# One more mixed pair in the turn of the FFN loop, and low parts made two chunks at a time

## What is computed

```
h = rmsnorm(x, norm_ffn_g[l])
x = x + (jax.nn.silu(h @ w_gate[l]) * (h @ w_up[l])) @ w_down[l]
return rmsnorm(x, norm_final_g)
```

## Time and profile before

| | |
|---|---|
| median of three runs | 1094.39 us |
| the profiled execution's own time | 1094.19 us |
| its span, first to last instruction | 1092.1 us |
| TensorE (PE) busy | 1080.7 us, 99% of the span |
| VectorE (DVE) busy | 936.1 us, 86% |
| ScalarE (ACT) busy | 601.1 us, 55% |
| mean granted clock of TensorE | 0.998 |
| chain that ended last | PE 80%, DVE 13%, DMA 3% |

### The profile page before, as it was taken

The page is one execution under the profiler, slowest core; times in us unless marked ns, Lnnn a source line. Parts: engine busy times, 40 slices in busy tenths (PEclk is TensorE's granted clock), DMA queues, the critical chain, the costliest instruction groups (busy, mean ns, idle before and its releaser), DMA issues.

```text
span 1092.1 us, 15574 instructions
## 1 busy us (share of the span) xinstructions
PE 1080.7 (99%) x5386; PEld 892.1 (82%) x5386; DVE 936.1 (86%) x1043; ACT 601.1 (55%) x738; POOL 189.9 (17%) x322
## 2 busy tenths in 40 slices
PE   9999999999999999999999999999999999999997
PEld 7878778888988888888888888888888888888886
DVE  7999998754875788989898998989899898989987
ACT  7569544445753565545555464655546465555544
POOL 7130143320100320311030302003030300303011
PEclk9999999999999999999999999999999999999999
DMA  9884588864665677666576666658566665757662
GB/s 360 286 232 147 179 235 242 268 191 150 212 218 187 205 221 229 214 206 212 197 230 220 185 228 204 201 191 241 200 210 214 207 206 182 229 192 231 214 213 113
DMA packets 123802, 232.18 MB, mean 213 GB/s; under 512 B 12016, under 2 KB 19568, under 8 KB 123120
## 3 DMA queue, kind: packets, MB, share of 16 engines
q1 hardware_dynamic: 113392, 215.10, 61.1%
q0 software_dynamic: 9952, 15.62, 5.4%
q10 hardware_dynamic: 416, 0.92, 0.2%
HBM read 218.09 MB, written 5.11 MB: 204 GB/s over the span
## 4 chain that ended last, share of the span: by engine, by line
PE 80%; DVE 13%; DMA 3%; issue 2%; ACT 1%; DVEq 0%; POOL 0%; SPq 0%; POOLq 0%; ACTq 0%
PE ps L1787 36%; PE ps L1751 31%; DVE w_lo L941 4%; PE ps L1778 3%; PE ps L1771 3%; PE ps L1775 3%; DMA raw<-in_w_in 2%; DVE w_lo L947 1%; DVE wb L1074 1%; DVE wb L1072 1%; ACT w_hi L544 1%; DVE wb_t L1073 1%; PE ps L2095 1%; PE ps L2096 1%; PE ps L2097 1%
## 5 line engine op out<-in xcount | busy, mean ns | idle before, releaser
L550 ACT ACTIVATE w_hi<-raw 128x1024 fp32r<-128x1024 f32 (+1 forms) x166 | 156.7, 955 | 191.2 <-PE ps L1787 117.7
L544 ACT ACTIVATE w_hi<-raw 128x1024 fp32r<-128x1024 f32 x135 | 142.7, 1060 | 154.0 <-DMA raw<-in_w_in 53.2
L941 DVE TENSOR_TENSOR w_lo<-raw,w_hi 128x1024 fp32r<-128x1024 f32 x136 | 163.8, 1220 | 63.7 <-ACT w_hi L544 63.1
L424 POOL DMA_DIRECT2D ff_moved<-ff_turned x184 | 97.0, 536 | 601.7 <-DVE ff_turned L1365 543.3
L947 DVE TENSOR_TENSOR w_lo<-raw,w_hi 128x1024 fp32r<-128x1024 f32 (+1 forms) x166 | 176.3, 1088 | 23.7 <-ACT w_hi L550 22.9
L550 ACT ACTIVATE w_hi<-raw_more 128x1024 fp32r<-128x1024 f32 x82 | 84.5, 1054 | 54.9 <-PE ps L1751 36.5
L947 DVE TENSOR_TENSOR w_lo<-raw_more,w_hi 128x1024 fp32r<-128x1024 f32 x82 | 97.4, 1218 | 8.4 <-ACT w_hi L550 8.4
L559 ACT ACTIVATE mix_hi<-mix 128x1024 fp32r<-128x1024 f32 x80 | 83.5, 1056 | 21.9 <-DVE mix L1312 15.2
L1323 DVE TENSOR_TENSOR mix_lo<-mix,mix_hi 128x2048 fp32r<-128x2048 f32 x40 | 91.4, 2285 | 0.0
L1751 PE MATMUL ps<-w_hi,ffT_hi 128*128 128x512 f32 x320 | 85.6, 389 | 0.0
L1751 PE MATMUL ps<-w_lo,ffT_hi 128*128 128x512 f32 x320 | 85.6, 389 | 0.0
(11 more groups left out here) (362 smaller groups left out, 2238.4 us busy)
## 6 DMA issues: line engine op xcount, KB each, us to landing
raw<-in_w_in SPq DMA_DIRECT2D x79, 512.0 KB, 5.4
raw<-in_w_gate SPq DMA_DIRECT2D x68, 512.0 KB, 3.9
raw<-in_w_up SPq DMA_DIRECT2D x68, 512.0 KB, 4.6
raw<-in_w_down SPq DMA_DIRECT2D x46, 512.0 KB, 4.1
raw_more<-in_w_down SPq DMA_DIRECT2D x42, 512.0 KB, 4.5
raw<-in_w_out SPq DMA_DIRECT2D x32, 512.0 KB, 4.1
raw_more<-in_w_gate SPq DMA_DIRECT2D x20, 512.0 KB, 4.5
raw_more<-in_w_up SPq DMA_DIRECT2D x20, 512.0 KB, 5.5
```

The lines of the kernel that those rows point to most:

```text
L424: eng.dma_start(moved[32 * b:32 * b + 32, :, a].rearrange("p t k j -> p t (k j)"), turned[32 * a:32 * a + 32, b].rearrange("p t k j -> p t ...
L544: nc.scalar.activation(w_hi[:, n % SPL], raw[:, n % RAW], ACT.Copy).then_inc(S["high_done"], 1)
L550: nc.scalar.activation(w_hi[:, c % SPL, at], raw_of(c)[:, at], ACT.Copy).then_inc(S["high_done"], 1)
L941: tt(w_lo[:, n % SPL], raw[:, n % RAW], w_hi[:, n % SPL].bitcast(F32), ALU.subtract).then_inc(S["low_done"], 1)
```

## The change

- `UNITS` becomes "CSCSSCSS": pair 7 is mixed too, so there are five mixed pairs and three plain ones, and a mixed pair is the last of the turn. The two slots of `mix_hi` and `mix_lo` go by `q % NM % 2`, so the first mixed pair of a turn takes the same slot as the last one of the turn before, and waits until that is free.
- The sums of h for pair 7 get a place of their own (`sD_hi`, `sD_lo`), `s_sum` gets two more blocks, and `combos` makes them for any mix of two pairs: for the last column two mixed pairs.
- The banks are numbered anew. Down columns 0 and 2 use P1's bank and bank 7, columns 1 and 3 those of P6 and P7 (`COL_BANKS`). Chunk 16 waits for ScalarE's copy of P1 (`p1_ready`), chunk 18 for the sums of P6 and P7 (`sum_step`). Pair 1 waits for the third add to `x2`, and only its second half for the fourth.
- `first_product` waits for the first half of the last mixed pair, pair 7, and `first_sums` waits for `mix_free` of that pair, which is given by its last matmul.
- `loop_low_two` makes the low parts of two chunks in one instruction of 128 x 2048 and then adds two to `low_done`. It is used for the plain pairs and for chunks 18 and 19, and 22 and 23.

```diff
-UNITS = "CSCSSCSC"
+UNITS = "CSCSSCSS"
...
-B_P2, B_P3, B_P4, B_P5, B_P1, B_P6, B_P7 = range(7)
+B_P2, B_P3, B_P4, B_P5, B_P6, B_P7, B_P1 = range(7)
+COL_BANKS = ((B_P1, 7), (B_P6, B_P7))
...
-             ("sC_hi", [P, 4, 2, P], F32R), ("sC_lo", [P, 4, 2, P], F32R)],
+             ("sC_hi", [P, 3, 2, P], F32R), ("sC_lo", [P, 3, 2, P], F32R), ("sD_hi", [P, 4, P], F32R), ("sD_lo", [P, 4, P], F32R)],
...
+        def combo_parts(c):
+
+            first, parts = 0, []
+            for u in (2 * c, 2 * c + 1):
+                width = 4 if u in MIXED else 2
+                to = [s_mixed[part][MIXED.index(u)] if u in MIXED else s_plain[part][PLAIN.index(u)] for part in range(2)]
+                parts.append((s_sum[:, first:first + width], to))
+                first += width
+            return parts
...
+        def column_psum(col):
+            a, b = COL_BANKS[col % 2]
+            return ps[:, a:b + 1]
...
                     if turn is not None and step == 1:
-                        act.wait_ge(S["mix_free"], count(turn, NM, q))
-                    nc.scalar.activation(mix_hi[:, q % 2, half_], mix[:, half_], ACT.Copy).then_inc(S["mix_high"], 1)
+                        act.wait_ge(S["mix_free"], count(turn, NM, q + (NM % 2 and q == NM)))
+                    nc.scalar.activation(mix_hi[:, q % NM % 2, half_], mix[:, half_], ACT.Copy).then_inc(S["mix_high"], 1)
...
             def first_product(j):
 
-                act.wait_ge(S["mix_free"], j * NM + (NM + 1))
+                act.wait_ge(S["pe_done"], j * TURN + (LOOP0 + 2 * MIXED[-1] + 1))
                 act.wait_ge(S["mix_low"], j * NM + NM)
...
             def first_sums(j):
 
                 dve.wait_ge(S["p1_ready"], j + 1)
+                dve.wait_ge(S["mix_free"], j * NM + (NM + 1))
                 tt(mix[:, 1], ps[:, B_P6], mix[:, 0], ALU.add).then_inc(S["sum_step"], 1)
...
+            def loop_low_two(c, turn=None):
+
+                dve.wait_ge(S["high_done"], count(turn, TURN, LOOP0 + c + 2))
+                s = c % SPL
+                tt(w_lo[:, s:s + 2], raw_pairs[c // 2 % (RING // 2)], w_hi[:, s:s + 2].bitcast(F32), ALU.subtract
+                   ).then_inc(S["low_done"], 2)
+
             def pair_low(c, turn=None):
 
-                loop_low(c, turn)
                 if mixed_pair(c):
+                    loop_low(c, turn)
                     loop_low(c + 1, turn, slice(NCOL, CK))
                     mix_low(c, turn)
                 else:
-                    loop_low(c + 1, turn)
+                    loop_low_two(c, turn)
...
                 first_sums(j)
                 last_sums(j)
-                loop_low(d + 2, j)
-                loop_low(d + 3, j)
+                loop_low_two(d + 2, j)
                 ff(j + 2)
...
                 loop_low(d + 5, j)
-                loop_low(d + 6, j)
-                loop_low(d + 7, j)
+                loop_low_two(d + 6, j)
                 down_add(j, 1)
...
+                if u == MIXED[0]:
+                    pe.wait_ge(S["cols_added"], turn * 4 + 8)
                 pe.wait_ge(S["mix_low"], count(turn, NM, q + 1))
...
                     if u == MIXED[0]:
                         pe.wait_ge(S["ff_ready"], j + 1)
-                        pe.wait_ge(S["cols_added"], j * 4 + 8)
+                        pe.wait_ge(S["cols_added"], j * 4 + 7)
...
                     if c == 2 * GRP:
                         pe.wait_ge(S["ffT_lo_ready"], j + 1)
+                        pe.wait_ge(S["p1_ready"], j + 1)
+                    if c == 2 * GRP + 2:
                         pe.wait_ge(S["sum_step"], j * 4 + 2)
```

More of the change, by code:

```diff
@@ L239, in build @@
             [("zT", [P, 8, SEQ], F32), ("sqT", [P, 8, SEQ], F32), ("y1T", [P, 8, SEQ], F32)],
-            [("mix_hi", [P, 2, 4, NCOL], F32R), ("mix", [P, 4, NCOL], F32), ("s_sum", [P, 6, P], F32)],
+            [("mix_hi", [P, 2, 4, NCOL], F32R), ("mix", [P, 4, NCOL], F32), ("s_sum", [P, 8, P], F32)],
             [("x_gain", [P, TOK, D_MODEL], F32)],
@@ L254, in build @@
             s_mixed[part] += [x[:, i] for i in range(2)]
+        for part in range(2):
+            s_mixed[part].append(s_last[part][:])
         wbT, dec, sT = (m[k] for k in ("wbT", "dec", "sT"))
@@ L572, in combo_high @@
                 act.wait_ge(S["s_summed"], c + 1)
-                i, k, _ = column_combos(c)
-                nc.scalar.activation(s_mixed[0][i], s_sum[:, 0:4], ACT.Copy).then_inc(S["s_hi"], 1)
-                nc.scalar.activation(s_plain[0][k], s_sum[:, 4:6], ACT.Copy).then_inc(S["s_hi"], 1)
+                for sums, (hi, _) in combo_parts(c):
+                    nc.scalar.activation(hi, sums, ACT.Copy).then_inc(S["s_hi"], 1)
             def xh(r):
@@ L1277, in combos @@
             def combos(c):
-                _, _, one = column_combos(c)
                 pair = h_sum[:].rearrange("p (u k) (t s) -> p u k t s", u=2, t=TOK)
-                (a11, a21), (a12, a22) = ([pair[:, one, k, t] for t in range(TOK)] for k in range(2))
-                plain = pair[:, 1 - one]
-                dve.wait_ge(S["h_summed"], 3 * c + 1)
+                done = sum(1 + 2 * (u in MIXED) for u in range(2 * c)) - c
+                dve.wait_ge(S["h_summed"], done + 1)
                 if c:
@@ L1285, in combos @@
                     dve.wait_ge(S["s_lo"], 2 * c)
[L1286 to L1292, removed]
+                mixed = []
@@ new lines, in combos @@
+                for i, (sums, _) in enumerate(combo_parts(c)):
+                    if 2 * c + i in MIXED:
+                        a11, a21, a12, a22 = (pair[:, i, k, t] for k in range(2) for t in range(TOK))
+                        tt(sums[:, 0], a21, a22, ALU.add).then_inc(S["h_summed"], 1)
+                        tt(sums[:, 2], a21, a11, ALU.subtract)
+                        mixed.append((sums, a11, a12))
+                    else:
+                        last = tt(sums, pair[:, i, :, 0], pair[:, i, :, 1], ALU.subtract)
@@ L1294, in combo_low @@
+                for i, (sums, a11, _) in enumerate(mixed):
+                    dve.wait_ge(S["h_summed"], done + 2 + i)
+                    tt(sums[:, 1], sums[:, 0], a11, ALU.subtract).then_inc(S["h_summed"], 1)
+                for i, (sums, _, a12) in enumerate(mixed):
+                    dve.wait_ge(S["h_summed"], done + 2 + len(mixed) + i)
+                    last = tt(sums[:, 3], a12, sums[:, 1], ALU.subtract)
+                last.then_inc(S["s_summed"], 1)
             def combo_low(c):
-                i, k, _ = column_combos(c)
@@ L1297, in combo_low @@
                 dve.wait_ge(S["s_hi"], 2 * c + 2)
-                tt(s_mixed[1][i], s_sum[:, 0:4], s_mixed[0][i].bitcast(F32), ALU.subtract).then_inc(S["s_lo"], 1)
-                tt(s_plain[1][k], s_sum[:, 4:6], s_plain[0][k].bitcast(F32), ALU.subtract).then_inc(S["s_lo"], 1)
+                for sums, (hi, lo) in combo_parts(c):
+                    tt(lo, sums, hi.bitcast(F32), ALU.subtract).then_inc(S["s_lo"], 1)
             def mix_sums(c, turn=None):
@@ L1322, in mix_low @@
                 dve.wait_ge(S["mix_high"], count(turn, 2 * NM, 2 * q + 2))
-                tt(mix_lo[:, q % 2], mix[:], mix_hi[:, q % 2].bitcast(F32), ALU.subtract).then_inc(S["mix_low"], 1)
+                tt(mix_lo[:, q % NM % 2], mix[:], mix_hi[:, q % NM % 2].bitcast(F32), ALU.subtract).then_inc(S["mix_low"], 1)
             def first_sums(j):
                 dve.wait_ge(S["p1_ready"], j + 1)
+                dve.wait_ge(S["mix_free"], j * NM + (NM + 1))
                 tt(mix[:, 1], ps[:, B_P6], mix[:, 0], ALU.add).then_inc(S["sum_step"], 1)
@@ L1378, in down_col @@
                 dve.wait_ge(S["cols_added"], before)
-                b0 = 6 - 2 * (c % 2)
                 cols = x2[:, :, NCOL * c:NCOL * (c + 1)]
-                tt(cols, ps[:, b0:b0 + 2], cols, ALU.add).then_inc(S["cols_added"], 1)
+                tt(cols, column_psum(c), cols, ALU.add).then_inc(S["cols_added"], 1)
             def side(n):
@@ L2112, in _ @@
                 ready(n)
-                column_chunk(n, n % SPL, act_pair(8 * part + 2 * i), 2 * (c % 2), i == 0, i == 3)
+                column_chunk(n, n % SPL, act_pair(8 * part + 2 * i), (2 * (c % 2), 2 * (c % 2) + 1), i == 0, i == 3)
                 side(n)
```

16 lines of the change are left out of this document (7 added, 9 removed).

## The result

The changed kernel takes **1110.51 us** (median of four, 1109.50 to 1111.75) beside 1094.10 for the kernel before: a ratio on record of 1.0143, interval 1.0131 to 1.0156 (the two medians alone give 1.0150). It is slower by 16.4 us; forecast were 1106 and a range of 1099 to 1111. The profiled execution took 1111.34 with a span of 1109.2, 17.1 over the span before.

What follows compares the result with a forecast made beforehand. TensorE bounded the kernel before; a VectorE loop was to pace the changed one: 6.71 + 10.88 + 1.29 + 45.14 = 64.02 us a turn against 62.84. Turn 0's +1.1 and nine turns' +10.6 gave +11.7, about 1106 us, range 1099 to 1111.

Steps and rivals of the forecast that it cites:

- the chain: From line 1328 (now 1348) to chunk 18's start: four sums 4.37, merged low part 2.29, hand-over 0.05, together 6.71 us.
- The stall at chunk 18: TensorE waits 1.47 us each turn for chunk 18's low part, ready at T + 6.86, wanted at T + 5.44.
- T: Start of TensorE's down stage (chunks 16 to 23); VectorE was forecast to reach line 1328 (now 1348) some 0.5 us later.
- The merged low part: Low parts of two chunks in one VectorE instruction: taken as 2.29 us alone, 2.20 to the next start, from mix_lo.
- VectorE's stretch: From the merged low part of chunks 24 and 25 to line 1328 (now 1348), VectorE without pause: 45.14 us.
- The rule against mergers: Broken-up instructions finish work sooner: separate lows would start chunk 18 some 1.07 us earlier; the opposite rule saves 0.07 each.
- The loop: Chunk 18 through chunk 21's end, VectorE's low part and back to line 1328: 64.02 us a turn, setting the pace.
- Rival 4: VectorE later still: deadlines of pairs 4 and 7 missed, gaps between instructions, 0.5 us a turn more, 1111 us; chance 0.12.
- covered by idle time like that before 419.10: Ahead of the loop: the extra column sums, some 0.3 us of VectorE, were to fall into idle time.
- Rival 5: The clock falls for the stalls: one chunk a turn at 1.2 GHz, 2.72 us more each, 1133 us; chance 0.03.
- The likeliest case: The forecast itself: a turn of 64.02 us set by the loop through VectorE, about 1106 us; chance 0.61.
- Rival 1: VectorE stays ahead and only TensorE's 0.68 us a turn shows: 1087.6 us, faster; chance 0.06.

Runs made afterwards that it cites:

- e8: Changed kernel with the low parts of pairs 0 and 2 in two instructions each again, chunks 18 and 19 still merged: 1104.83 us.
- e1: Changed kernel with the low parts of chunks 18 and 19 in two instructions again, nothing else: 1099.21 us.
- e3: Changed kernel with the low parts of the next turn's pair 0 (chunks 24 and 25) in two instructions again: 1108.39 us.
- e2: Changed kernel with all five merged low parts in two instructions each again, leaving the fifth mixed pair alone: 1095.19 us.
- e4: Kernel before, pair 7 still plain, with merged low parts for its four plain pairs, chunks 18, 19 and 22, 23: 1096.22 us.
- e9: Kernel before with merged low parts for its plain pairs and chunks 22, 23, but chunks 18 and 19 separate: 1095.12 us.
- e6: Changed kernel reordered: merged low 18, 19 before the sums, chunk 20's high part before SiLU, pairs 0 and 2 separate: 1087.97 us.
- e5: Changed kernel with the merged low part of chunks 18 and 19 made ahead of the four sums, nothing else: 1109.70 us.

## Why the prediction was right, and where it was short

**What bounds, and the chain.** The stall at chunk 18 behind sums and merged low part was forecast at 1.47 with TensorE leading and is 1.48 there (e8); in the changed kernel line 1348 starts 0.39 after T, not 0.5. The chain itself was summed to 6.71 and is 6.72 (604.60 to 611.32). The merged low part, priced from mix_lo, takes 2.28 (608.98 to 611.26). VectorE's stretch from the low part of chunk 24 to line 1348, forecast 45.14, is 668.88 - 623.71 = 45.17.

**The rule against mergers.** The Trainium skill (Perfetto Trace Analysis, Optimizing Scalar/DVE Operations) gave two opposite rules. The one on broken-up instructions is what the runs follow (e1: 11.3 us back). The saving by the other, forecast 0.07 an instruction, shows in the start-to-start times (2.20 for 634.71 to 636.91, 2.27 before), and bought nothing. The Trainium skill (VectorE: DVE Perf Modes, The TRN2 errata) has a formula for a float32 addition of two tensors that gives 2.29 us for 2048 elements, an estimate, and the trace agrees for this subtraction: 2.28 to 2.29.

**The loop, step mis-sized.** Forecast 64.02 a turn, measured 64.33 (64.28 in the turn shown). The term that was short is the one from chunk 18's start to VectorE's low part of chunk 24: 10.88 + 1.29 = 12.17 was taken from a TensorE that doesn't start behind a wait; it is 12.39 (611.32 to 623.71), of which 0.15 is in the matmuls. The other 0.07 lies between the start of chunk 22 and VectorE's low part (622.35 to 623.71, 1.36 where 1.29 was taken). Over nine turns this (2.0), 0.03 a turn in VectorE's stretch (0.3) and 0.47 us that line 1356 idled once in the last turn make 2.8 us. That a second loop of the same length (pair 2, e3) lay under the first was not seen; it doesn't alter the time, but made an experiment fail.

**Rival 4** (VectorE later still, 1111) came nearer to the time than the forecast did, but not by its cause. Its missed deadlines of pairs 4 and 7 are there, and cost the weight loads up to 0.3 us each; yet VectorE's own stretch is 45.17 of 45.14, so they don't lengthen the loop. What did is the term above.

**The turn ahead.** The passes begin at 478.8, 0.8 later than the forecast gives (476.9 + 1.1 = 478.0). The step that failed is "covered by idle time like that before 419.10": the sums for pair 7 belong to the last column, behind that idle time.

```profile
428.27 0.69 DVE L1318 TENSOR_TENSOR sB_lo<-s_sum,sB_hi 128x512 fp32r<-128x512 f32 x1
428.87 0.69 DVE L1318 TENSOR_TENSOR sD_lo<-s_sum,sD_hi 128x512 fp32r<-128x512 f32 x1
429.67 2.29 DVE L1490 TENSOR_TENSOR w_lo<-raw,w_hi 128x2048 fp32r<-128x2048 f32 x1
432.84 1.23 DVE L1331 TENSOR_TENSOR mix<-raw 128x1024 f32<-128x1024 f32 x1 [0.87 <-DMA raw<-in_w_up]
```

Pair 0's low part starts at 429.67; it was 428.83 in the kernel before. Of the 0.84, 0.37 is there already when the last low part ahead of these starts (427.12, 426.75 before; it waits for ScalarE's high part, which stands behind the sums and their high part, 0.61 where it was 0.40), and 0.47 comes behind it, 0.27 of that by the longer low part of the sums (0.69, where it was 0.42). The mergers aren't the cause: in e2, which has none, pair 0's low part starts at 429.69. And e4 and e9, which have the mergers without the fifth mixed pair, begin at 476.6 and 477.4.

**The clock.** Rival 5 had the right mechanism and the wrong place: the clock stayed at 2.4 GHz through nine stalls of 1.5 us and fell once, behind the last turn's stall. That stall was the longest, 2.03 us, since line 1356 came 0.47 late. Of the 1.8 us that the end behind the last pass of line 1359 is longer (51.4 against 49.6), the clock is 1.55, the slow start 0.15 and 0.1 is the start of chunk 18 behind that pass. In e3, with 1.69 of idle at the same place and no half clock, the time behind the last pass is 49.8. Only one of the four executions of the changed kernel left a trace. Their mean granted clocks, 0.997, 0.999, 0.999 and 0.998 for 1111.34, 1109.69, 1109.50 and 1111.75 us, would fit a fall in the two slower ones and none in the two quicker; that isn't shown, and from what idle on it falls stays open.

**The sum.** +0.8, +2.8 and +1.8 are the 5.4 us between the forecast span of 1103.8 and the 1109.2 measured. The likeliest case, with its chain, its loop and its pace setter, was the one that came. That the time stayed inside the range, by 0.5 us, is luck as far as these three go: none of them had been named, and what covered them was the width left for rival 4, whose cause didn't come.

**Rival 1**, the saving alone, was a matter of order, not of work: its 1087.6 is what e6 reaches.

## What to carry to other kernels

Ask of every merged or moved instruction which deadline stands right behind it: the merger saves 0.07 us, but its first half's result comes 1.07 later (e1 against the changed kernel), and behind a chain of sums that was worth 1.1 us a turn. An engine with work for 98% of a turn can keep up if no instruction stands ahead of one that is wanted sooner; so put the low part that TensorE wants next ahead of sums that nobody waits for yet, and fill SiLU's time with work that doesn't need it. Look for the second loop before opening the first: a wait taken away is only worth the distance to the next one (e3 gave 2.1 us of an expected 3.5 to 6.5).

## What the runs showed of the hardware

- **A wait that TensorE meets costs more than its length.** The first four matmuls behind one take 1.01 to 1.05 us to the next start instead of 0.91, even if it was missed by 0.03 us (e4). Weight loads otherwise run ahead of the matmuls, at chunk 18 of the kernel before by 0.23 us (606.37, the matmul at 606.60); behind the wait of the changed kernel it is 0.01 (611.31 and 611.32). That this missing run-ahead is the cause of the slow start is argued, not shown.

```profile
606.37 0.87 PEld L1751 LDWEIGHTS ps<-w_hi,ffT_hi 128*128 128x128 f32 x4
```
```profile
611.31 0.76 PEld L1775 LDWEIGHTS ps<-w_hi,ffT_hi 128*128 128x128 f32 x4 [1.93 <-DVE w_lo L1490]
```

- **The clock at short stalls.** Stalls of 1.5 us each turn left the granted clock at 1.00 for nine turns. The longest one of the last turn ended in a stretch at mostly 1.2 GHz in two profiles (changed, 2.03 us idle; e5, 2.55), and not in e3 (1.69).
- Line 1356 idled 0.47 us behind line 1350 in the last turn of the changed kernel's profile (1.16 us from start to start, 0.73 in its loop turns). In the last turn of e1, e3, e5 and e8, with the same two lines, it is 0.79 or 0.80, so the pause isn't one of the written-out copy. Its cause is open.
